# Eight tiles of a modulation's matrix-vector product on GpSimd instead of VectorE

## Chip, cores and metric

The kernel runs on one core of a Trainium2 chip. The metric is the device time in microseconds of one execution. Before the change it is 2267.84 us (median of three runs, 2267.05 to 2270.59).

## What is computed

Two transformer blocks run one after the other on 512 tokens of width 1024, in float32. The first block has two layers. Each layer begins with a modulation of a condition vector `c`:

```python
cond = jax.nn.silu(c)
for i in range(DEPTH):                       # 2 layers
    mod = (cond @ ada_w[i] + ada_b[i])[:, None, :]
    sh1, sc1, g1, sh2, sc2, g2 = jnp.split(mod, 6, axis=-1)
    h = rmsnorm(x, norm1_g[i]) * (1.0 + sc1) + sh1
    y = attention(h)                         # layer 0: sliding window, 16 query heads, 2 key heads
    x = x + g1 * y
    h = rmsnorm(x, norm2_g[i]) * (1.0 + sc2) + sh2
    x = x + g2 * swiglu(h, w_gate[i], w_up[i], w_down[i])
```

The second block (a gated convolution, a state space scan and a gated MLP) is not touched by the change.

## The kernel before

**Matrix products.** TensorE does each float32 product with three fp32r matmuls (lines 875, 877, 879): weight and activation are split into a high part, made by ScalarE (`whi`, line 1263), and a low part, made by VectorE (`wlo`, line 1572). The weights come as 360 units of 128x1024 through three buffers each of `raw`, `whi` and `wlo`. SyncE's queue loads `raw` (line 2090).

**The modulation.** There are 12 vectors of 1024 (`MODS`), j = 0 to 11, each the sum of 8 products of a 128x1024 tile of `ada_w` with a column of `cond`. A tile is n = 8j + k. Vectors 0 and 1 are made at the start by TensorE. The others (n = 16 to 95) are made by VectorE in `fma`: the first tile of a vector by a `tensor_scalar` (line 1587, output = tile x cond[k]), the others by a `scalar_tensor_tensor` (line 1590, acc = tile x cond[k] + acc). `modsum` (line 917) then sums over the partitions on TensorE, `modrows` copies the row on ScalarE, `modturn` (line 927) turns it to a column, `modadd` (lines 1612, 1617) adds the bias. j = 2 is `g1`, j = 3 and 4 are `sh2` and `sc2`, which the second norm needs. The accumulators are two: even j in slots 29 and 30, odd j in 31 and 32, so the first tile of a vector must wait until `modsum` has read the vector two before it. The tiles arrive in six buffers (`ada`, line 2103), and the load of a tile waits until the tile six before it has been multiplied.

**The order of work.** `score()` writes one list of ticks; each engine runs through it and does the ticks that are its own, in this order, waiting on semaphores. `mods()` yields one tile a step. Six tiles are woven into the first projection, 16 into the first attention (`queries()`), two into its output projection, the rest into the first MLP. In `queries()` there are 16 visits, two for each pair of heads t = 0 to 7; they are called visit 0 to 15 here. A visit runs, each for another item in flight, `exps`, `scores`, `turned`, `values`, then takes one tile from `mods()`; an even visit ends with `query` of the next t. Between two visits TensorE has three or four steps of a projection. On VectorE:
- `scores` adds the mask and takes the maxima (line 1832), then makes the negative maximum (lines 1836, 1838), for which ScalarE's `exps` (line 1436) waits. When the maxima are taken, the PSUM banks of the scores come free, and TensorE takes them again for what follows;
- `turned` of an odd visit: lines 1850, 1852, 1857 (a copy of the reciprocal denominators into a 128x512 tile);
- `values`: lines 1865 and 1568;
- `query`: line 1788 (head statistics from PSUM), then the rotation in lines 1798, 1802, 1804.

GpSimd takes the power -0.5 of those head statistics (line 2036) as soon as line 1788 is done, and later adds up the squares for the norms (line 2045).

Of the kernel before, what the change touches and what calls it, by code (L numbers as in the profile page):

```python
# [12 lines left out]
ALU = mybir.AluOpType  # L13
# [4 lines left out]
KD = D // P  # L18
# [7 lines left out]
NADA = 6  # L26
# [6 lines left out]
NEG = -1.0e30  # L33
EPS1 = 1e-6
EPS2 = 1e-5
MODS = [(0, 1), (0, 0), (0, 2), (0, 3), (0, 4), (0, 5)] + [(1, j) for j in range(6)]


# [61 lines left out]
class Score:  # L100
# [5 lines left out]
    def tick(self, *t):  # L106
        self.ticks.append(t)
# [93 lines left out]
def score():  # L201
    s = Score()
    tick, gemm = s.tick, s.gemm

    def column_sums(*js):

        tick("modsum", js)
        s.soon(3, "modrows", js)
        s.soon(7, "modturn", js)
        s.soon(9, "modadd", js)  # L210

    def mods():
        for j in range(2, 12):
            for k in range(KD):
                if k == 3 and j in (3, 6):
                    column_sums(j - 1)
                tick("fma", 8 * j + k)
                yield 1
            if j == 7:
                column_sums(6, 7)  # L220
                yield 1

# [65 lines left out]
    mod = mods()  # L288
# [364 lines left out]
def program(nc, ctx, io, ticks):  # L653
    def signal(name, by=1):
        return Signal(ctx.enter_context(nc.semaphore(name)), by)
# [13 lines left out]
        signal(f"a_{n}") for n in ("cut", "half", "ev", "sq", "att", "stick", "ssd"))  # L669
    v_cut, v_half, v_ev, v_mod, v_norm, v_res, v_att, v_stick, v_ssd, v_conv = (  # L670
        signal(f"v_{n}") for n in ("cut", "half", "ev", "mod", "norm", "res", "att", "stick", "ssd", "conv"))
    p_sum, p_pow, p_rope, p_ssd = (signal(f"p_{n}") for n in ("sum", "pow", "rope", "ssd"))
    sums_dram = nc.dram_tensor("sums", (32, S), F, kind="Internal").ap()
    ya_dram = nc.dram_tensor("ya", (KD, P, S), F, kind="Internal").ap()

# [175 lines left out]
    def tensor(e):  # L851
# [59 lines left out]
        def modsum(js):  # L911
            b = take(("mod", js))
            for n, j in enumerate(js):
                w.wait_ge(v_mod, ("fma", 8 * j + 7))
                for half in range(2):
                    g = 64 * n + 32 * half
                    i = e.matmul(b[g:g + 32, :], C("one").to_broadcast([P, 32]), modacc[j][:, S * half:S * half + S], start=True, stop=True,
                                 skip_group_check=True)
            i.then_inc(*t_mod.up(*js))
            give(("mod", js), a_att, ("modrows", js))  # L920
# [335 lines left out]
    def scalar(e):  # L1256
# [288 lines left out]
        for name, *a in ticks:  # L1545
            if name in do:
                do[name](*a)

    def item(n):

        return n // 8, n % 8 // 2, n % 2
# [11 lines left out]
    def vector(e):  # L1563
# [16 lines left out]

        def fma(n):
            j, k = divmod(n, KD)
            a, o = ada[(n - 16) % NADA], modacc[j]
            w.wait_ge(d_ada[(n - 16) % NADA], n)
            if k == 0:
                w.wait_ge(*((t_mod, j - 2) if 3 < j < 10 else (a_att, "cond")))
                e.tensor_scalar(o, a, cond[:, 0:1], None, ALU.mult).then_inc(*v_mod.up(("fma", n)))
            else:
                w.wait_ge(v_mod, ("fma", n - 1))
                e.scalar_tensor_tensor(o, a, cond[:, k:k + 1], o, ALU.mult, ALU.add).then_inc(*v_mod.up(("fma", n)))  # L1590
# [397 lines left out]
    def gpsimd(e):  # L1988
        w = Waits(e)
        TWO_PI = 2.0 * np.pi  # L1990
        C1 = 6.28125
        C2 = float(np.float32(round((TWO_PI - C1) * 2 ** 19) / 2 ** 19))
        C3 = float(TWO_PI - C1 - C2)
        MAGIC = 12582912.0
        LIM = 3.1415925
        steps = [0]

        def next_step(op):

            op.then_inc(*p_rope.up(steps[0]))  # L2000
            w.wait_ge(p_rope, steps[0])
            steps[0] += 1

        def reduce_angle(x, k, scale, shift):
            next_step(e.tensor_scalar(k, x, scale / TWO_PI, shift, ALU.mult, ALU.add))
            next_step(e.tensor_scalar(k, k, MAGIC, None, ALU.add))
            next_step(e.tensor_scalar(k, k, -MAGIC, None, ALU.add))
            for c in (C1, C2, C3):
                next_step(e.tensor_scalar(part, k, -c / scale, None, ALU.mult))
                next_step(e.tensor_tensor(x, x, part, ALU.add))  # L2010

        def angles():
            blocks = lambda ap: ap.rearrange("p (c r) -> p c r", c=4)
            w.wait_ge(d_in, "vec")
            w.wait_ge(d_pos, "pos")
            next_step(e.tensor_copy(part[:, 0:4], pos[:, :]))
            next_step(e.tensor_tensor(blocks(ang), blocks(C("invf")), part[:, 0:4].unsqueeze(2).to_broadcast([P, 4, 8]), ALU.mult))
            reduce_angle(ang, turn, 1.0 / 4096, 0.0)
            next_step(e.tensor_copy(ang2, ang))
            reduce_angle(ang2, turn, 1.0, 0.25)  # L2020
            next_step(e.tensor_scalar(ang2, ang2, float(np.pi / 2), None, ALU.add))

        def sine():
            reduce_angle(ang, turn, 1.0, 0.0)
            e.tensor_scalar(ang2, ang2, LIM, -LIM, ALU.min, ALU.max).then_inc(*p_rope.up("cos"))
            e.tensor_scalar(ang, ang, LIM, -LIM, ALU.min, ALU.max).then_inc(*p_rope.up("sin"))

        def pow_(sid):
            v, r = stat[sid]
            w.wait_ge(v_norm, ("scaled", sid))  # L2030
            e.tensor_tensor(r, v, C("half", 0, 4), ALU.pow).then_inc(*p_pow.up(sid))

        def head_pow(t):
            v, r = qstat[t]
            w.wait_ge(v_att, ("qstat", t))
            e.tensor_tensor(r, v, C("half", 0, 8), ALU.pow).then_inc(*p_pow.up(("q", t)))

        def add(sid, d):
            if 0 < d < nstat(sid):
                if d == 1:  # L2040
                    w.wait_ge(a_sq, (sid, 0))
                else:
                    w.wait_ge(p_sum, (sid, d - 1))
                w.wait_ge(a_sq, (sid, d))
                e.tensor_tensor(acc, acc, sq_of(sid, d), ALU.add).then_inc(*p_sum.up((sid, d)))  # L2045

        def sq(sid, d, last):
            if sid:
                add(sid, d)

        def per_head(ap, c, g):
            o = 32 * c + 8 * g
            return ap[:, o:o + 8].unsqueeze(2).to_broadcast([P, 8, 64])

        def h8(ap):
            return ap.rearrange("p (h r) -> p h r", h=8)

        def xrow(g, c):
            if c < 3:
                w.wait_ge(v_ssd, ("xd", g, c))  # L2060
                w.wait_ge(a_ssd, "dec")
                if g:
                    w.wait_ge(t_ssd, ("state", g - 1, c))
                e.tensor_tensor(h8(STMP[c]), h8(XD[c]), per_head(dec, c, g), ALU.mult).then_inc(*p_ssd.up(("st", g, c)))

        def masked(g, h):
            ex = EX[(8 * g + h) % 6]
            w.wait_ge(a_ssd, ("ex", g, h))
            w.wait_ge(a_ssd, ("x", 20 + g))
            e.tensor_tensor(ex[:, P:], ex[:, P:], Ct[g % 2][:, P:], ALU.mult).then_inc(*p_ssd.up(("ex", g, h)))  # L2070

        do = {"angles": angles, "sine": sine, "pow": pow_, "kstat": lambda: head_pow("k"), "query": head_pow, "sq": sq,
              "gadd": lambda i: add(("g", i // 4), i % 4), "xrow": xrow, "masked": masked}
        for name, *a in ticks:
            if name in do:
                do[name](*a)
# [2 lines left out]

    def sync(e):  # L2080
        w = Waits(e)
        loaded = [0, 16]

        def load():
            u = loaded[0]
# [6 lines left out]
        def ada_in(n):  # L2092
            j, k = divmod(n, KD)
            l, jj = MODS[j]
            return io["ada_w"][l, k * P:(k + 1) * P, jj * D:(jj + 1) * D]

        def fma(n):
            while loaded[1] < min(96, n + NADA):
                q = loaded[1]
                loaded[1] += 1  # L2100
                if q >= 16 + NADA:
                    w.wait_ge(v_mod, ("fma", q - NADA))
                e.dma_start(ada[(q - 16) % NADA], ada_in(q)).then_inc(*d_ada[(q - 16) % NADA].up(q))

        def evac(tile):
            if tile[0] == "spill":
# [40 lines left out]
                e.dma_start(early_part(q, k).rearrange("p (j c) -> p j c", j=2), parts[:, :, 256 * q:256 * q + 256]).then_inc(  # L2147
                    *d_early[q, k].up("in"))
        e.dma_start(cst[:, soon:], io["consts"][:, soon:]).then_inc(*d_late.up("in"))
        fma(13)  # L2150
        load()
        load()
        fma(16)
        def dtgain():
            w.wait_ge(v_mod, ("fma", 93))
            e.dma_start(wdt, io["wdt"]).then_inc(*d_wdt.up("in"))

        do = {"dtgain": dtgain, "lower": lambda u: load() if u > 2 else None, "fma": fma, "evac": evac, "dtturn": dtturn, "decay": lambda g, h: row(8 * g + h + 1), "fetch": fetch, "final": final}
        for name, *a in ticks:
            if name in do:  # L2160
                do[name](*a)
# [2 lines left out]
    engines = tensor, scalar, vector, gpsimd, sync  # L2164
    signals = [d_in, d_pos, d_out, *d_x, *d_raw, *d_ada, *d_early.values(), d_late, *d_ya, *d_row, d_sums, d_wdt, t_mm, t_mod, t_norm, t_att, t_stick, t_ssd, a_cut, a_half,
               a_ev, a_sq, a_att, a_stick, a_ssd, v_cut, v_half, v_ev, v_mod, v_norm, v_res, v_att, v_stick, v_ssd, v_conv, p_sum,
               p_pow, p_rope, p_ssd]
    for engine in engines:
        engine(Dry())
    for s in signals:  # L2170
# [89 lines left out]
```

## Time and profile before

| | |
|---|---|
| median of the runs | 2267.84 us |
| the profiled execution | 2267.9 us |
| its span, first to last instruction | 2265.9 us |
| TensorE busy | 2232.9 us (99%) |
| VectorE busy | 1193.5 us (53%) |
| ScalarE busy | 895.2 us (40%) |
| GpSimd busy | 165.0 us (7%) |
| granted TensorE clock, mean | 0.996 |

The time of the execution is 2.0 us longer than its span. "Busy" of TensorE counts pipelined matmuls whose ends are modelled, so what its rows show well are the gaps between them. A time such as 145.15 is in microseconds from the start of the span. "<-" behind a row names what released the instruction.

### The profile page before, as it was taken

To read this page: it belongs to the slowest core of one execution; us is meant where nothing else is said; L and a number is where in the kernel's file an instruction comes from. 1 tells how busy PE (TensorE), PEld (TensorE's weight loads), DVE (VectorE), ACT (ScalarE), POOL (GpSimd) and SP (SyncE) were. 2 spreads that over 40 slices of the span, in tenths; PEclk is the share of its full clock that TensorE was granted. 3 is DMA by queue.
4 is the path that set the end of the run, shared out by engine and by line. 5 is a ranking of instruction groups with operands and counts; after the bars stand their busy time and mean duration, and the time that the engine had idled before them with its cause. 6 is when DMAs were issued, how large, how long until landed. Compare 5 with 4: busy or idle time off the path is not lost. (4 is left out here: it accounts for less than half of the span.)

```text
span 2265.9 us, 26906 instructions
## 1 busy us (share of the span) xinstructions
PE 2232.9 (99%) x10904; PEld 1793.3 (79%) x10904; DVE 1193.5 (53%) x1651; ACT 895.2 (40%) x1445; POOL 165.0 (7%) x147
## 2 busy tenths in 40 slices
PE   8999999999999999999999999999999999999998
PEld 6766888888777778888888877887788888888886
DVE  4775755643465754333337446567752447553453
ACT  4654332223354533322333236367742224331331
POOL 2112000000000010000001001032210001000001
PEclk9999999999999999999999999999999999999999
DMA  9432555632212112232222324333333232333222
GB/s 332 149 121 84 215 212 207 215 108 93 84 57 75 57 68 94 93 103 102 94 84 98 107 75 154 103 103 112 102 114 115 84 111 85 102 94 102 93 84 84
DMA packets 82171, 258.72 MB, mean 114 GB/s; under 512 B 8800, under 2 KB 17376, under 8 KB 82048
## 3 DMA queue, kind: packets, MB, share of 16 engines
q1 hardware_dynamic: 82048, 257.01, 33.3%
q8 instruction: 86, 1.41, 0.3%
q14 instruction: 37, 0.30, 0.0%
HBM read 252.71 MB, written 4.26 MB: 113 GB/s over the span
## 5 line engine op out<-in xcount | busy, mean ns | idle before, releaser
L875 PE MATMUL pb<-hhi,whi 128*128 128x512 f32 x1936 | 767.3, 396 | 2.0 <-ACT hhi L1301 2.0
L877 PE MATMUL pb<-hhi,wlo 128*128 128x512 f32 x1936 | 754.3, 390 | 2.7 <-DVE wlo L1572 2.7
L879 PE MATMUL pb<-hlo,whi 128*128 128x512 f32 x1936 | 754.7, 390 | 0.0
L1572 DVE TENSOR_TENSOR wlo<-raw,whi 128x1024 fp32r<-128x1024 f32 x360 | 446.0, 1243 | 544.4 <-ACT whi L1263 544.3
L1263 ACT ACTIVATE whi<-raw 128x1024 fp32r<-128x1024 f32 x360 | 379.1, 1057 | 699.9 <-PE pb L879 675.3
L875 PEld LDWEIGHTS pb<-hhi,whi 128*128 128x128 f32 x1936 | 363.5, 188 | 88.3 <-issue 15.8
L877 PEld LDWEIGHTS pb<-hhi,wlo 128*128 128x128 f32 x1936 | 363.8, 188 | 78.9 <-DVE wlo L1572 4.1
L879 PEld LDWEIGHTS pb<-hlo,whi 128*128 128x128 f32 x1936 | 363.4, 188 | 77.9 <-DVE hlo L1669 1.3
L875 PE MATMUL pb<-ahi,whi 128*128 128x512 f32 x848 | 334.1, 394 | 1.6 <-ACT ahi L1459 0.9
L877 PE MATMUL pb<-ahi,wlo 128*128 128x512 f32 x848 | 330.2, 389 | 1.1 <-DVE wlo L1572 1.1
L879 PE MATMUL pb<-alo,whi 128*128 128x512 f32 x848 | 330.5, 390 | 0.0
L875 PEld LDWEIGHTS pb<-ahi,whi 128*128 128x128 f32 x848 | 159.2, 188 | 37.3 <-issue 4.2
L877 PEld LDWEIGHTS pb<-ahi,wlo 128*128 128x128 f32 x848 | 159.3, 188 | 34.4 <-DVE wlo L1572 1.5
L879 PEld LDWEIGHTS pb<-alo,whi 128*128 128x128 f32 x848 | 159.2, 188 | 34.1 <-DVE alo L1568 0.8
L2045 POOL TENSOR_TENSOR slab<-slab 128x512 f32<-128x512 f32 x46 | 69.4, 1508 | 1558.2 <-ACT slab L1280 1557.2
L1692 DVE SCALAR_TENSOR_TENSOR slab<-slab,vec 128x509 f32<-128x509 f32 (+2 forms) x132 | 99.0, 750 | 4.7
L1568 DVE TENSOR_TENSOR alo<-slab,ahi 128x512 fp32r<-128x512 f32 x90 | 62.3, 692 | 68.7 <-ACT ahi L1379 50.5
L1590 DVE SCALAR_TENSOR_TENSOR slab<-slab,small 128x1024 f32<-128x1024 f32 x70 | 90.6, 1295 | 1.9 <-DVE slab L1590 0.5
L1725 DVE TENSOR_TENSOR slab<-slab,pb 128x512 f32<-128x512 f32 x66 | 45.0, 683 | 47.6 <-PE pb L879 47.5
L1379 ACT ACTIVATE ahi<-slab 128x512 fp32r<-128x512 f32 x66 | 41.7, 632 | 68.7 <-DVE slab L1725 68.7
L1280 ACT ACTIVATE slab<-X 128x512 f32<-128x512 f32 x48 | 30.2, 629 | 82.7 <-DVE X L1701 35.0
L1877 DVE TENSOR_TENSOR_SCAN slab<-slab,cst 128x128 f32<-128x128 f32 (+3 forms) x64 | 52.2, 815 | 6.3 <-ACT slab L1472 6.3
(258 smaller groups left out, 1729.8 us busy)
## 6 DMA issues: line engine op xcount, KB each, us to landing
raw<-stream SPq DMA_DIRECT2D x360, 512.0 KB, 3.3
slab<-ada_w SPq DMA_DIRECT2D x80, 512.0 KB, 5.1
early<-ada_w SPq DMA_DIRECT2D x32, 256.0 KB, 8.1
slab<-sums SPq DMA_DIRECT2D x32, 256.0 KB, 4.2
X<-xT SPq DMA_DIRECT2D x8, 256.0 KB, 5.0
ya<-slab SPq DMA_DIRECT2D x8, 256.0 KB, 4.1
slab<-ya SPq DMA_DIRECT2D x8, 256.0 KB, 5.3
outT<-X SPq DMA_DIRECT2D x8, 256.0 KB, 2.1
```

Source lines behind the costliest of these rows:

```text
L875: e.matmul(out, wh, hi, start=s.k == 0, stop=False)
L877: e.matmul(out, wl, hi, start=False, stop=False)
L879: i = e.matmul(out, wh, lo, start=False, stop=s.last)
L1263: e.activation(whi[:, u % NW, :], raw[:, u % NRAW, :], ACT.Copy).then_inc(*a_cut.up(u))
L1379: e.activation(a_out[f % HALF][0], SG[f % 6], ACT.Copy).then_inc(*a_half.up(("f", l, f)))
L1568: e.tensor_tensor(out, src, hi.bitcast(F), ALU.subtract).then_inc(*v_half.up(key))
L1572: e.tensor_tensor(wlo[:, u % NW, :], raw[:, u % NRAW, :], whi[:, u % NW, :].bitcast(F), ALU.subtract).then_inc(*v_cut.up(u))
L1590: e.scalar_tensor_tensor(o, a, cond[:, k:k + 1], o, ALU.mult, ALU.add).then_inc(*v_mod.up(("fma", n)))
L1692: e.scalar_tensor_tensor(t[:, d:], u[:, :S - d], W(name, (width - 1 - d) * tiles + i), t[:, d:], ALU.mult, ALU.add).then_inc(*v_conv.up((k ...
L1725: e.tensor_tensor(t, t, b, ALU.mult).then_inc(*v_ev.up(tile))
L1877: e.tensor_tensor_scan(p[:, 0:wd][:, ::-1], RS[n % 4][:, 0:wd][:, ::-1], C("late", S - wd)[:, 0:wd][:, ::-1], 1.0, ALU.mult, ALU.max).then ...
L2045: e.tensor_tensor(acc, acc, sq_of(sid, d), ALU.add).then_inc(*p_sum.up((sid, d)))
```

## The change

The tiles n = 24 to 31 (j = 3) are made by GpSimd in a new tick `pool_fma`. Its first tile is one `tensor_scalar`; each other tile is a `tensor_scalar` in place in the `ada` buffer, a wait, and a `tensor_tensor` add into the accumulator. The order of the tiles becomes `MOD_ORDER`: 16 to 26, then 32, 27, 33, 28, 34, 29, 35, 30, 36, 31, 37, 38, 39, and then as before. So visits 2, 3, 4, 6, 8, 10, 12 and 14 of the attention take a GpSimd tile, and visits 0, 1, 5, 7, 9, 11, 13, 15 one of VectorE (22, 23, 32, 33, ... 37). As the first tile of j = 4 (n = 32) now comes in visit 5, the column sum of j = 2 moves from tile 27 to tile 26, and its copy follows after one product instead of three. Buffers and loads follow the place in `MOD_ORDER`.

```diff
+MOD_ORDER = [*range(16, 27), 32, 27, 33, 28, 34, 29, 35, 30, 36, 31, 37, 38, 39, *range(40, 96)]
...
     def column_sums(*js):
         tick("modsum", js)
-        s.soon(3, "modrows", js)
+        s.soon(1 if js == (2,) else 3, "modrows", js)
...
     def mods():
-        for j in range(2, 12):
-            for k in range(KD):
-                if k == 3 and j in (3, 6):
-                    column_sums(j - 1)
-                tick("fma", 8 * j + k)
-                yield 1
-            if j == 7:
+        for n in MOD_ORDER:
+            j, k = divmod(n, KD)
+            if n == 26 or n == 51:
+                column_sums(2 if n == 26 else 5)
+            tick("pool_fma" if j == 3 else "fma", n)
+            yield 1
+            if n == 63:
                 column_sums(6, 7)
                 yield 1
...
-                w.wait_ge(v_mod, ("fma", 8 * j + 7))
+                w.wait_ge(*multiplied(8 * j + 7))
...
+    def multiplied(n):
+        return (p_mod if n // KD == 3 else v_mod), ("fma", n)
...
+        def pool_fma(n):
+            j, k = divmod(n, KD)
+            at = MOD_ORDER.index(n) % NADA
+            a, o = ada[at], modacc[j]
+            w.wait_ge(d_ada[at], n)
+            if k == 0:
+                w.wait_ge(a_att, "cond")
+                e.tensor_scalar(o, a, cond[:, 0:1], None, ALU.mult).then_inc(*p_mod.up(("fma", n)))
+            else:
+                e.tensor_scalar(a, a, cond[:, k:k + 1], None, ALU.mult).then_inc(*p_mod.up(("scaled", n)))
+                w.wait_ge(p_mod, ("scaled", n))
+                e.tensor_tensor(o, o, a, ALU.add).then_inc(*p_mod.up(("fma", n)))
...
         def fma(n):
-            while loaded[1] < min(96, n + NADA):
-                q = loaded[1]
+            ada_load(MOD_ORDER.index(n) + NADA)
+
+        def ada_load(places):
+            while loaded[1] < min(len(MOD_ORDER), places):
+                place = loaded[1]
                 loaded[1] += 1
-                if q >= 16 + NADA:
-                    w.wait_ge(v_mod, ("fma", q - NADA))
-                e.dma_start(ada[(q - 16) % NADA], ada_in(q)).then_inc(*d_ada[(q - 16) % NADA].up(q))
+                q = MOD_ORDER[place]
+                if place >= NADA:
+                    w.wait_ge(*multiplied(MOD_ORDER[place - NADA]))
+                e.dma_start(ada[place % NADA], ada_in(q)).then_inc(*d_ada[place % NADA].up(q))
```

## Rows read from the trace of the kernel before

**Rows 1.** Busy time by stretch: us, PE, PEld, DVE, ACT, POOL, clock, DMA, GB/s
```profile
57.00:135.00 78.00, 77.87 (x518) 56.85 (x517) 61.37 (x174) 49.73 (x130) 14.06 (x7) 1.00 0.42 148
135.00:180.00 45.00, 39.67 (x275) 29.29 (x276) 30.17 (x95) 29.16 (x80) 4.02 (x2) 1.00 0.30 105
```
**Rows 2.** What TensorE waited for between 135 and 180 us (total, times, longest)
```profile
PE pb L1077 <- DVE small L1832: 3.2, 3, 1.1
PE pb L1063 <- DVE small L1832: 1.2, 2, 0.6
```
**Rows 3.** Timeline of TensorE: start, us, operation, idle before and its releaser
```profile
145.15 0.88 PE L1077 MATMUL pb<-slab 128*64 128x128 f32 x12 [1.10 <-DVE small L1832]
...
155.78 1.10 PE L1006 MATMUL pb<-slab,cst 128*128 128x512 f32 x2
...
170.14 1.13 PE L1049 MATMUL pb<-slab 64*128 64x256 f32 x8
...
200.84 1.05 PE L917 MATMUL pb<-slab,cst 128*32 128x512 f32 x4 [1.26 <-DVE slab L1590]
```
**Rows 4.** Timeline of VectorE in visits 9 to 15
```profile
129.02 0.16 DVE L1788 TENSOR_SCALAR small<-pb 128x8 f32<-128x8 f32 x1
...
132.51 0.16 DVE L1836 SCALAR_TENSOR_TENSOR small<-small 128x4 f32<-128x4 f32 x1
...
141.32 0.75 DVE L1587 TENSOR_SCALAR slab<-slab,small 128x1024 f32<-128x1024 f32 x1
...
155.85 1.28 DVE L1590 SCALAR_TENSOR_TENSOR slab<-slab,small 128x1024 f32<-128x1024 f32 x1
...
157.72 0.68 DVE L1802 TENSOR_TENSOR slab<-pb,slab 128x512 f32<-128x512 f32 x1
...
170.92 1.28 DVE L1590 SCALAR_TENSOR_TENSOR slab<-slab,small 128x1024 f32<-128x1024 f32 x1
172.12 0.41 DVE L1832 CUSTOM_DVE_ANT_0 slab<-pb,cst 128x256 f32<-128x256 f32 x1
```
**Rows 5.** Timeline of ScalarE: the exponentials of visit 9, a weight cut
```profile
132.91 0.60 ACT L1436 ACTIVATE slab<-slab,small 128x256 f32<-128x256 f32 x1 [3.04 <-DVE small L1838]
...
149.01 1.06 ACT L1263 ACTIVATE whi<-raw 128x1024 fp32r<-128x1024 f32 x1 [4.33 <-PE pb L879]
```
**Rows 6.** Timelines of GpSimd and of SyncE's queue in visits 8 and 9
```profile
129.25 2.01 POOL L2036 TENSOR_TENSOR small<-small,cst 128x8 f32<-128x8 f32 x1 [13.05 <-DVE small L1788]
...
128.31 1.14 SPq L2103 DMA_DIRECT2D slab<-ada_w  x2
```
**Rows 7.** By line: count, duration in ns min/median/max, first and last start
```profile
L2045 POOL TENSOR_TENSOR slab<-slab x46: 1277/1299/2163, 196.2 to 2248.1; 128x512 f32<-128x512 f32 x46
...
L2070 POOL TENSOR_TENSOR slab<-slab x17: 1002/1020/1990, 1390.0 to 1652.8; 128x384 f32<-128x384 f32 x17
...
L2009 POOL TENSOR_SCALAR slab<-slab x9: 287/288/718, 5.8 to 20.1; 128x32 f32<-128x32 f32 x9
...
L1617 DVE SCALAR_TENSOR_TENSOR small<-small,vec x3: 169/169/740, 208.3 to 603.1; 128x8 f32<-128x8 f32 x3
...
L1798 DVE TENSOR_TENSOR slab<-slab x8: 677/680/682, 63.9 to 157.1; 128x512 f32<-128x512 f32 x8
...
L1651 DVE SCALAR_TENSOR_TENSOR hlo<-X,vec,hhi x16: 751/1272/1550, 1180.6 to 1897.0; 128x512 fp32r<-128x512 f32 x16
```
**Rows 8.** Timelines of VectorE and GpSimd where both work on SBUF
```profile
208.32 0.74 DVE L1617 SCALAR_TENSOR_TENSOR small<-small,vec 128x8 f32<-128x8 f32 x1
...
207.29 1.74 POOL L2045 TENSOR_TENSOR slab<-slab 128x512 f32<-128x512 f32 x1 [3.14 <-ACT slab L1280]
...
1183.41 1.28 DVE L1651 SCALAR_TENSOR_TENSOR hlo<-X,vec,hhi 128x512 fp32r<-128x512 f32 x1 [1.44 <-ACT hhi L1284]
...
1182.84 1.30 POOL L2045 TENSOR_TENSOR slab<-slab 128x512 f32<-128x512 f32 x1 [337.31 <-ACT slab L1280]
```

More of the change, by code:

```diff
@@ L671, in program @@
         signal(f"v_{n}") for n in ("cut", "half", "ev", "mod", "norm", "res", "att", "stick", "ssd", "conv"))
-    p_sum, p_pow, p_rope, p_ssd = (signal(f"p_{n}") for n in ("sum", "pow", "rope", "ssd"))
+    p_sum, p_pow, p_rope, p_ssd, p_mod = (signal(f"p_{n}") for n in ("sum", "pow", "rope", "ssd", "mod"))
     sums_dram = nc.dram_tensor("sums", (32, S), F, kind="Internal").ap()
@@ L1582, in fma @@
             j, k = divmod(n, KD)
-            a, o = ada[(n - 16) % NADA], modacc[j]
-            w.wait_ge(d_ada[(n - 16) % NADA], n)
+            at = MOD_ORDER.index(n) % NADA
+            a, o = ada[at], modacc[j]
+            w.wait_ge(d_ada[at], n)
             if k == 0:
@@ L2036, in head_pow @@
             e.tensor_tensor(r, v, C("half", 0, 8), ALU.pow).then_inc(*p_pow.up(("q", t)))
+        def pool_fma(n):
+            j, k = divmod(n, KD)
+            at = MOD_ORDER.index(n) % NADA
+            a, o = ada[at], modacc[j]
+            w.wait_ge(d_ada[at], n)
+            if k == 0:
[5 more added lines that the diff above has]
+                e.tensor_tensor(o, o, a, ALU.add).then_inc(*p_mod.up(("fma", n)))
         def add(sid, d):
@@ L2070, in masked @@
             e.tensor_tensor(ex[:, P:], ex[:, P:], Ct[g % 2][:, P:], ALU.mult).then_inc(*p_ssd.up(("ex", g, h)))
-        do = {"angles": angles, "sine": sine, "pow": pow_, "kstat": lambda: head_pow("k"), "query": head_pow, "sq": sq,
+        do = {"angles": angles, "sine": sine, "pow": pow_, "kstat": lambda: head_pow("k"), "query": head_pow, "pool_fma": pool_fma, "sq": sq,
               "gadd": lambda i: add(("g", i // 4), i % 4), "xrow": xrow, "masked": masked}
@@ L2081, in sync @@
         w = Waits(e)
-        loaded = [0, 16]
+        loaded = [0, 0]
         def load():
@@ L2149, in sync @@
         e.dma_start(cst[:, soon:], io["consts"][:, soon:]).then_inc(*d_late.up("in"))
-        fma(13)
+        ada_load(3)
         load()
         load()
-        fma(16)
+        ada_load(NADA)
         def dtgain():
@@ L2156, in dtgain @@
             e.dma_start(wdt, io["wdt"]).then_inc(*d_wdt.up("in"))
-        do = {"dtgain": dtgain, "lower": lambda u: load() if u > 2 else None, "fma": fma, "evac": evac, "dtturn": dtturn, "decay": lambda g, h: row(8 * g + h + 1), "fetch": fetch, "final": final}
+        do = {"dtgain": dtgain, "lower": lambda u: load() if u > 2 else None, "fma": fma, "pool_fma": fma, "evac": evac, "dtturn": dtturn, "decay": lambda g, h: row(8 * g + h + 1), "fetch": fetch, "final": final}
         for name, *a in ticks:
@@ L2166, in program @@
                a_ev, a_sq, a_att, a_stick, a_ssd, v_cut, v_half, v_ev, v_mod, v_norm, v_res, v_att, v_stick, v_ssd, v_conv, p_sum,
-               p_pow, p_rope, p_ssd]
+               p_pow, p_rope, p_ssd, p_mod]
     for engine in engines:
```

## The prediction

> **What bounds the kernel now.** I read the busy times first. TensorE is busy nearly all the time, so an edit on VectorE can only win what TensorE stands idle for on its account. The table by stretch shows where that is. From 57 to 135 us TensorE is busy 77.87 of 78 us; from 135 to 180 us, when the output projection has begun, it is busy 39.67 of 45 us [rows 1]. The 5.3 us between are the most that the visits can give. TensorE's waits in that stretch name VectorE: 3.2 us before `values` and 1.2 us before `turned`, both released by the maxima of line 1832 [rows 2]. TensorE's timeline puts the three large ones in visits 11, 13 and 15, each about 1.1 us, the first at 145.15 [rows 3]. The banks of the scores are free only when the maxima are taken, and in odd visits VectorE is late with these: ahead of them it does, in one row, the tile of the even visit, line 1788 and the rotation [rows 4]. One more idle of TensorE belongs to the modulation: 1.26 us before `modsum` of j = 3 and 4 at 200.84, released by tile 39 [rows 3]. Tile 39 stays on VectorE, so this wait stays.
>
> **What the change takes away.** VectorE loses eight tiles: tile 24, a `tensor_scalar` of 0.75 us, and seven of 1.28 us; visit 5 changes from a long to a short one and visit 10 loses a short one. That is some 9 us of VectorE's work. What counts is what lies ahead of the three waits.
> - Visit 10 loses 0.75 us, 0.66 to the start of the next instruction (141.32, [rows 4]). TensorE's wait in visit 11 shrinks by 0.66 us.
> - Visit 12 loses 1.28 us at 155.85. But the rotation there needs TensorE's turn, which ends at 155.78 + 1.10 = 156.88 [rows 3]; line 1802 started at 157.72 [rows 4], so the row of work moves up by 0.8 us at most.
> - Visit 14 loses 1.28 us at 170.92. The maxima behind it began at 172.12 [rows 4]; their scores end at 170.14 + 1.13 = 171.27 [rows 3]. That is 0.8 us.
>
> Sum: 0.66 + 0.8 + 0.8 = 2.3 us gained. The tiles of visits 2 to 8 win nothing: TensorE did not wait there [rows 1].
>
> **What the change adds on GpSimd.** The add: 128x384 takes 1.00 us and 128x512 takes 1.28 us undisturbed [rows 7], which is 2.15 ns a column; 1024 columns are 1.28 + 512 x 0.00215 = 2.4 us. The `tensor_scalar` of 1024 columns is not in the trace. Its lower bound is the 0.29 us of 32 columns [rows 7], its upper the add's 2.4 us. It reads 1024 elements a partition, as many as an add of 512 columns does, so I take the 1.3 us of that row. A tile then costs GpSimd some 3.8 us, between 2.7 and 4.8. The Trainium skill, page GPSIMD Engine Reference, section "Engine selection", says that one-input operations on GpSimd are roughly line-rate; by that an estimate would be 0.9 us for the scaling and 3.3 us for the tile. No run so far shows it.
>
> GpSimd has nothing else to do between two powers, which lie 13 us apart [rows 6], and its tile is loaded long before: the loads at 128.31 [rows 6] are for tiles five places ahead. So it does not keep to its visit; each tile starts right behind the power of line 2036, one visit or more early (two tiles, 7.6 us, behind the second power). No power is made late, and SyncE's loads, which now wait for GpSimd's tiles of six places before, find them done. I cost both at nothing; if a tile took over 10 us the powers would become late and with them the scores.
>
> **What it costs VectorE.** The two engines get in each other's way. At 208.32 a `scalar_tensor_tensor` of 8 columns on VectorE takes 0.74 us and not 0.17, and ends as the add on GpSimd ends that started at 207.29 [rows 7, 8]. At 1183.41 line 1651 takes 1.28 us, not 0.75, beside an add that ran from 1182.84 [rows 7, 8]: VectorE stood until about 0.2 us before the add's end, then did its 0.75 us. So a VectorE instruction with two SBUF inputs that meets a running add waits for all of it. The powers do not do this: line 1798 runs beside each of them and always takes 0.68 us [rows 7].
>
> Now place it. Line 1788 of visit 8 starts at 129.02 and moves to 127.8. The power runs to 130.1, the scaling to 131.4, the add to 133.9. Line 1836, two SBUF inputs, stood at 132.51 [rows 4] and would come at 131.3, line 1838 at 131.5: one of the two meets the scaling's end or the add. The negative maximum, for which ScalarE's exponentials were already waiting at 132.91 [rows 5], comes between 132.5 and 134, so between 0.4 us earlier and 1.2 later; I take +0.8. ScalarE's chain behind it (exponentials, evacuations, weight cut) feeds VectorE's line 1572, and so the wait of visit 11: +0.8 us. The same pattern follows in visit 11, where the stall of 2.2 us (an add less 0.2) meets slack: ScalarE stood there until 149.01 for TensorE anyway [rows 5]; the VectorE tile behind it is late, and I put +0.3 on TensorE. In visit 13 the exponentials again follow the negative maximum at once; 2.2 us less the 0.8 moved up, with 0.4 of slack before the next bank is wanted: +1.0. After visit 14 GpSimd has no tile left. Sum: 0.8 + 0.3 + 1.0 = 2.1 us lost.
>
> The Trainium skill, page SBUF — State Buffer, section "Who interferes with whom", says that a copy or a `tensor_scalar` on VectorE that runs in a two-port mode blocks in the same way. By that, line 1857 and the tiles of line 1587 would stall as well; no row here shows one beside a GpSimd add. As line 1857 stands behind line 1836, it would mostly come after the same add, and the sum would move by at most one more stall.
>
> **Other edits.** The column sum of j = 2 comes two visits earlier, into the stretch where TensorE has no wait; its tiles are ready, its four matmuls are the same. It shifts which PSUM bank follows which; bounded by +-0.6 us, the size of one bank wait in [rows 2], taken as zero. Tile 32 needs that sum to have been read, a visit earlier: no wait.
>
> **The sum.** -2.3 + 2.1 = -0.2 us on the profiled execution, 2267.9 us, which stands 0.06 us above the median of the runs. Forecast 2267.7 us.
>
> **Rivals.**
> - *Traded evenly* (forecast): each stall of VectorE eats what the removed tile gave. 2266.0 to 2270.0 with the bounds of the scaling and of the overlaps. Chance 0.62.
> - *VectorE wins the ports*: its short instructions slip in between and GpSimd waits. Then only the 2.3 us stay: 2265.6. For it: the powers never disturb. Against it: all of [rows 8]. Chance 0.15.
> - *The lock on the path* (slower): in visits 9, 11 and 13 the add always starts before line 1836, and nothing hides it. 3 x 2.2 - 2.3 = +4.3 us, 2272.2; with the scaling (1.1 us each) blocking as well, +7.6 us, 2275.5. It decides from the point where GpSimd's scaling ends before VectorE's maxima do. For it: ScalarE waits on exactly this value [rows 5]. Against it: slack in visit 11. Chance 0.15.
> - *VectorE's lateness was all*: with 9 us less work, all 5.3 us of idle in 135 to 180 go: 2262.6. Against it: the bounds by TensorE's own turn and scores above. Chance 0.04.
> - *It does not do what it says*: GpSimd's tiles take so long that powers or `modsum` wait for them; over 10 us a tile, some 2270 and more. Chance 0.04.
>
> **How the numbers follow.** A measurement of this kernel tells about 0.2%, 4.5 us, from no change. The first two cases and the lower half of the third are within it. Faster by more: the fourth, 0.04. Slower by more: half of the third and part of the last, 0.09. Same: 0.87. The range takes in the first two cases and the nearer end of the third, and a margin for the runs' own spread (2267.05 to 2270.59): 2264.0 to 2272.5.
>
> **What the profile after would show.** VectorE busy without stalls would fall by 9 us; with mine it falls less, as stalled rows count as busy. Rows of lines 1836, 1838, 1850 or 1857 longer than 0.5 us show the lock; if all stay at 0.17, the second case holds. GpSimd's tiles should start right behind the powers, with adds of 2.4 us or more. The wait of visit 15 should shrink to 0.3 us; those of 11 and 13 hardly in sum. I am wrong if TensorE gets new waits before 135 us, or if the powers move.

## The result, and the profile after

The changed kernel takes **2278.12 us** (median of 6 runs, 2277.23 to 2280.42). The kernel before took 2269.14 us beside it. The ratio is 1.0038, with a 95% interval of 1.0028 to 1.0048: the change costs 9 us. The forecast was 2267.7 us, within 2264.0 to 2272.5, and was wrong. The profiled execution took 2280.42 us, its span is 2278.5 us.

First the same two stretches as in [rows 1] and three short ones (window, length, busy time of TensorE, its weight loads, VectorE, ScalarE and GpSimd, granted clock, share of the DMA engines, GB/s):

```profile
57.00:135.00 78.00, 73.37 (x460) 53.55 (x460) 57.45 (x150) 45.30 (x118) 35.99 (x15) 0.98 0.37 129
135.00:180.00 45.00, 38.76 (x264) 27.97 (x263) 35.86 (x94) 24.28 (x68) 21.89 (x9) 0.94 0.32 111
123.00:129.00 6.00, 6.00 (x35) 4.12 (x31) 3.67 (x9) 2.10 (x4) 1.45 (x1) 0.72 0.00 0
153.00:159.00 6.00, 5.01 (x24) 3.88 (x24) 5.79 (x14) 0.53 (x1) 5.34 (x3) 0.72 0.55 218
179.00:185.00 6.00, 6.00 (x31) 4.61 (x29) 2.20 (x7) 3.91 (x10) 0.00 (x0) 0.77 0.30 102
```

Before the change TensorE stood idle 0.1 us of the first stretch [rows 1]; now it stands 4.6 us there. The granted clock, 1.00 in both stretches of [rows 1], is 0.72 to 0.77 in three windows of 6 us: part of each ran at the lower of the two levels, 1.2 GHz. What TensorE waited for from 57 to 250 us, largest first (total, times, longest):

```profile
PE pb L1078 <- DVE small L1618: 3.4, 1, 3.4
PE pb L1064 <- DVE small L1838: 2.9, 2, 2.3
PE pb L1078 <- DVE small L1838: 1.8, 3, 1.1
PE pb L918 <- DVE slab L1596: 1.2, 1, 1.2
PE pb L1078 <- ACT spare L1324: 1.2, 1, 1.2
```

Lines 1064, 1078 and 1838 are 1063, 1077 and 1832 of before. Two names are new against [rows 2]: line 1618, `modadd`, which adds the bias to a column sum, and line 1324, `modrows`, which copies its row. Both waits belong to the column sum of j = 2, not to GpSimd. TensorE's timeline places them:

```profile
98.36 1.05 PE L918 MATMUL pb<-slab,cst 128*32 128x512 f32 x4
...
104.66 0.88 PE L1078 MATMUL pb<-slab 128*64 128x128 f32 x12 [1.21 <-ACT spare L1324]
...
114.44 0.46 PE L928 MATMUL pb<-cst,spare 64*128 64x64 f32 x4
...
122.36 0.88 PE L1078 MATMUL pb<-slab 128*64 128x128 f32 x12 [3.43 <-DVE small L1618]
123.16 0.50 PE L876 MATMUL pb<-hhi,whi 128*128 128x512 f32 x1
123.50 0.40 PE L878 MATMUL pb<-hhi,wlo 128*128 128x512 f32 x1
123.73 0.57 PE L880 MATMUL pb<-hlo,whi 128*128 128x512 f32 x1
124.10 0.63 PE L876 MATMUL pb<-hhi,whi 128*128 128x512 f32 x1
...
153.99 1.09 PE L1078 MATMUL pb<-slab 128*64 128x128 f32 x12 [1.10 <-DVE small L1838]
...
169.80 0.88 PE L1078 MATMUL pb<-slab 128*64 128x128 f32 x12 [0.46 <-DVE small L1838]
...
177.15 0.65 PE L1064 MATMUL pb<-cst,slab 128*128 128x128 f32 x4 [2.31 <-DVE small L1838]
...
212.96 1.05 PE L918 MATMUL pb<-slab,cst 128*32 128x512 f32 x4 [1.25 <-DVE slab L1596]
```

The bank that `modsum` filled at 98.36 is wanted again by `values` of visit 5, before ScalarE has copied the row. The bank that `modturn` filled at 114.44 is wanted by `values` of visit 7, before VectorE has added the bias. And 1.7 us after this 3.43 us wait the product that took 0.40 us takes 0.63: the granted clock fell to the lower level after TensorE had stood. Why the bias comes so late is in the timeline of VectorE and GpSimd in visit 7:

```profile
118.85 0.42 DVE L1838 CUSTOM_DVE_ANT_0 slab<-pb,cst 128x256 f32<-128x256 f32 x1
...
119.11 2.84 POOL L2053 TENSOR_SCALAR slab<-slab,small 128x1024 f32<-128x1024 f32 x1
...
120.34 0.17 DVE L1842 SCALAR_TENSOR_TENSOR small<-small 128x4 f32<-128x4 f32 x1
120.54 0.17 DVE L1844 TENSOR_TENSOR small<-small 128x4 f32<-128x4 f32 x1
...
121.13 1.10 DVE L1863 COPY spare<-small 128x512 f32<-128x512 f32 x1
122.03 2.42 POOL L2055 TENSOR_TENSOR slab<-slab 128x1024 f32<-128x1024 f32 x1
122.15 0.15 DVE L1618 TENSOR_TENSOR small<-pb,vec 128x8 f32<-128x8 f32 x1
122.22 3.31 DVE L1596 SCALAR_TENSOR_TENSOR slab<-slab,small 128x1024 f32<-128x1024 f32 x1
```

In VectorE's order the bias stands behind the rotation, the maxima and the copy of a whole visit, and comes 7.7 us after the turn. In the kernel before it comes at 126.61, 4.0 us after the turn at 122.60, and the rotation's first step (line 1788) follows at 129.02 [rows 4]. GpSimd adds little to it: the copy took 1.10 us instead of 0.43. The tile product behind it met the add and took 3.31 us instead of 1.28, but TensorE has no further wait until 145.50.

**The balance.** Executions differ by some 1.6 us before the first visit, so I count from the first head statistics (line 999) to `modsum` of j = 3 and 4 (the last of TensorE's rows above): 62.09 to 212.96, 150.87 us. In the kernel before it is 60.40 to 200.84, 140.44 us. Up to 132.89 (125.18 before) the difference is 6.0 us: the waits of 1.2 and 3.4 us, and 1.5 us for seven products at the lower clock (0.43 us apart, not 0.23) and the scores behind them. Behind it are another 4.4 us: two more low stretches after the waits at 153.99 and 177.15 (1.3 and 0.9 us), new waits of 0.9 and 1.7 us (the second is the 2.31 in the place of 0.59), less gains of 0.6 and 0.8 us at visits 13 and 15. That is 3.4 us. Another 0.9 us is the lower clock again, in the matmuls that stand between these two waits and the products (at 153.99 line 1078 takes 1.09 us, at 169.80 the same shape 0.88). The last 0.2 us has no row. The median of the runs shows 9 us and not 10.4: the profiled execution is the slowest of the six.

### The profile page after: what moved, and what is told of

The parts are those of the page before. It is cut to its first block and busy times, and to the rows that moved or that the text cites. A ratio compares the mean times of both kernels' runs of the same rounds, so it can differ in the third digit from the quotient of the medians.

```text
span 2278.5 us, 26908 instructions
## 1 busy us (share of the span) xinstructions
PE 2240.0 (98%) x10904; PEld 1797.8 (79%) x10904; DVE 1201.3 (53%) x1643; ACT 895.0 (39%) x1445; POOL 204.7 (9%) x162
```

## The experiments

My theory after the result: the earlier column sum costs the time, by its two bank waits. The rival: GpSimd's work costs it, by holding up VectorE's instructions.

**The change without GpSimd, and GpSimd without the new order.** In e1 VectorE makes all tiles, in the changed order:

```diff
-            tick("pool_fma" if j == 3 else "fma", n)
+            tick("fma", n)
```

> The new order of tiles and the moved column sum, but all tiles on VectorE. Theory A (the moved column sum): the two new waits of TensorE, 3.4 us for the bank that the bias addition of j = 2 frees and 1.2 us for the bank that its row copy frees, stay or grow by the tile that is back on VectorE; 2273 to 2276 us, against about 2269 for the kernel before. Theory B (GpSimd's lock on the ports): no GpSimd tile, so no loss; 2268 to 2270 us.

In e2 GpSimd makes j = 3, but the tiles, the column sum and its steps are in the order of before:

```diff
-MOD_ORDER = [*range(16, 27), 32, 27, 33, 28, 34, 29, 35, 30, 36, 31, 37, 38, 39, *range(40, 96)]
+MOD_ORDER = [*range(16, 96)]
...
-            if n == 26 or n == 51:
+            if n == 27 or n == 51:
...
-        s.soon(1 if js == (2,) else 3, "modrows", js)
+        s.soon(3, "modrows", js)
```

> GpSimd makes j = 3, but the tiles keep the order of before and the column sum of j = 2 stays at tile 27. A: the new bank waits are gone; 2267 to 2271 us. B: the stalls of copies and tiles beside GpSimd stay where visits 3 to 9 have them; if these are the cause, 2273 to 2278 us.

Measured: e1 2280.0 us, ratio 1.0042 (1.0027 to 1.0057). e2 2271.62 us, 1.0005 (0.9996 to 1.0014). The whole loss is there without GpSimd and gone with it in the old order. The rival falls as the cause of the loss. e1 came out 4 us above its expectation: beside the two waits, now 4.0 and 1.2 us, a third one grew (1.5 us on line 1794 for 0.4 in the changed kernel), and the granted clock from 135 to 180 us is 0.92, not 0.94.

**Which part of the new order.** e5 is the kernel before with one edit: the column sum of j = 2 one tile earlier (with its row after one product).

> The order of tiles of before and all tiles on VectorE; only the column sum of j = 2 (sum, copy, turn, bias addition) comes one tile earlier, as in the changed kernel. If this move alone makes the loss, TensorE waits 1.2 us and about 4 us for its two banks and the time is 2277 to 2281 us. If the loss needs the new order of tiles too, under 2274 us.

Measured: 2277.73 us, 1.0033 (1.0020 to 1.0046). So this one edit costs 7.5 us (4.5 to 10.4), most of the loss if not all. Its waits and its clock in TensorE's timeline:

```profile
106.48 0.88 PE L1078 MATMUL pb<-slab 128*64 128x128 f32 x12 [1.21 <-ACT spare L1324]
...
124.70 1.34 PE L1078 MATMUL pb<-slab 128*64 128x128 f32 x12 [3.95 <-DVE small L1618]
125.97 0.80 PE L876 MATMUL pb<-hhi,whi 128*128 128x512 f32 x1
```

From the first head statistics to those of visit 10 it needs 85.00 us (63.90 to 148.90), before 78.41 (60.40 to 138.81). That is 6.6 us more, and the rows account for it: waits 1.21 + 3.95, and 1.55 for the seven groups from 124.70 to 128.55, which take 3.85 us and not the 2.30 of before.

**Which step of the sum.** e3 is the changed kernel with the turn and the bias later; e6 has the bias earlier instead, right behind the turn.

```diff
-        s.soon(7, "modturn", js)
-        s.soon(9, "modadd", js)
+        s.soon(11 if js == (2,) else 7, "modturn", js)     # e3
+        s.soon(13 if js == (2,) else 9, "modadd", js)      # e3
+        s.soon(7 if js == (2,) else 9, "modadd", js)       # e6, turn unchanged
```

> The changed kernel with one edit: the turn and the bias addition of j = 2 come four products later, at the place that they had before. A: the 3.4 us wait goes, and with it the stretch at the lower TensorE clock behind it (about 1.5 us); 2272 to 2274 us. B: no change, 2277 to 2279 us.

> The changed kernel, with the bias addition of j = 2 in the list right behind its turn, ahead of the rotation and the maxima of visit 7, instead of two products later. If TensorE waits for a bank that this short VectorE instruction frees, the 3.4 us wait goes and the time is 2271 to 2274 us, as with the later turn; if it is the turn's own place on TensorE that costs, it stays at 2277 us or more.

Measured: e3 2272.47 us, 1.0012 (1.0003 to 1.0021); e6 2273.48 us, 1.0013 (1.0004 to 1.0023). Either edit takes the wait on line 1618 away and gives back about 5 us, more than the 3.4 us of the wait. The granted clock of both profiles is 1.00 from 97 to 137 us, where the changed kernel's is 0.96. So it is the place of the bias in VectorE's order that costs, and not the place of the turn in TensorE's.

**What GpSimd's work costs.** From e3, three kernels. e7 shrinks the GpSimd tiles 25 to 31 to 8 columns, e8 only their scalings. e4 stands on the changed kernel and puts a second scaling in the place of the add. In these three the vector j = 3 is not the sum of its tiles.

```diff
-                e.tensor_scalar(a, a, cond[:, k:k + 1], None, ALU.mult)...
+                e.tensor_scalar(a[:, 0:8], a[:, 0:8], cond[:, k:k + 1], None, ALU.mult)...        # e7, e8
-                e.tensor_tensor(o, o, a, ALU.add)...
+                e.tensor_tensor(o[:, 0:8], o[:, 0:8], a[:, 0:8], ALU.add)...                      # e7
+                e.tensor_scalar(o, a, cond[:, k:k + 1], None, ALU.mult)...                        # e4
```

> The kernel with the later turn (2272.5 us), and GpSimd's tiles 25 to 31 shrunk from 1024 to 8 columns (j = 3 is then not the sum of its tiles; tile 24 stays whole): VectorE is relieved and nothing is blocked. The difference to the kernel with the later turn is the whole price of GpSimd's port use. If that is what eats the gain: 2267 to 2269.5 us, 3 to 5 us below it. If the blocking is hidden: 2271.5 us or more.

> The kernel with the later turn, with GpSimd's scalings of tiles 25 to 31 shrunk to 8 columns and the adds whole (j = 3 is then wrong). The adds now start right behind the powers, 2.9 us earlier, and meet line 1842 (1836 before), the negative maximum. If a stall there is worse than one behind it, as the prediction had it, above 2272.5 us; if only the length of the blocking counts, 2269 to 2272 us.

> The changed kernel, with GpSimd's add replaced by a second scaling into the accumulator (j = 3 is then not the sum of its tiles). Tells what a scaling blocks. If a running scaling blocks VectorE instructions with two SBUF inputs, as the page says of every GpSimd instruction that reads SBUF, VectorE's tiles 33 to 36 take 3.7 us each, longer than the 3.3 us beside the add, and the time stays 2277 to 2280 us. If it blocks only copies and tensor_scalar, as the rows of the changed kernel look, the tiles take 1.28 us, the 2.3 us wait of visit 14 shrinks to under 1 us, and the time is 2275 to 2277 us.

Measured: e7 2267.93 us, 0.9989 (0.9979 to 0.9998); e8 2268.61 us, 0.9992 (0.9982 to 1.0001); e4 2274.43 us, 1.0019 (1.0009 to 1.0028). With e3 at 2272.47, GpSimd's work costs 4.5 us against e7; the adds alone cost 0.7, which the intervals don't resolve. So the offload would be worth 2.75 us (0.5 to 4.8 by the interval) if GpSimd stalled nobody, where the first term of the forecast has 2.3. Six of the seven adds of e8 fall where the forecast had put its stalls, on the negative maximum, which then takes 1.3 to 1.6 us. VectorE and GpSimd in e8:

```profile
131.46 2.39 POOL L2055 TENSOR_TENSOR slab<-slab 128x1024 f32<-128x1024 f32 x1
...
132.29 1.57 DVE L1842 SCALAR_TENSOR_TENSOR small<-small 128x4 f32<-128x4 f32 x1
133.90 0.17 DVE L1844 TENSOR_TENSOR small<-small 128x4 f32<-128x4 f32 x1
```

The scaling ahead of the add moves the add 2.9 us later, away from the small instructions and onto the large ones. This is how the changed kernel gets its 2.31 us wait in visit 14 (VectorE and GpSimd in the changed kernel):

```profile
170.90 0.83 DVE L1863 COPY spare<-small 128x512 f32<-128x512 f32 x1
...
171.54 2.44 POOL L2055 TENSOR_TENSOR slab<-slab 128x1024 f32<-128x1024 f32 x1
...
171.66 3.41 DVE L1577 TENSOR_TENSOR wlo<-raw,whi 128x1024 fp32r<-128x1024 f32 x1
174.98 1.27 DVE L1596 SCALAR_TENSOR_TENSOR slab<-slab,small 128x1024 f32<-128x1024 f32 x1
...
176.26 0.28 DVE L1838 CUSTOM_DVE_ANT_0 spare<-pb,cst 128x128 f32<-128x128 f32 x1
```

The weight split takes 3.41 us and not 1.22. The maxima of the next visit stand behind it and free their banks late. In e4, which has no add, this wait is 0.9 us, and e4 came out below both of its expectations.

**Can the scaling be had elsewhere?** e9 is e3 with ScalarE scaling the tiles, one tile ahead, and GpSimd only adding. e10 is e3 with `modrows` right behind `modsum`. e11 has both.

```diff
+        def prescale(n):                                                                  # e9, e11
...
+            e.activation(a, a, ACT.Copy, scale=cond[:, n % KD:n % KD + 1])...
...
-        s.soon(1 if js == (2,) else 3, "modrows", js)
+        tick("modrows", js) if js == (2,) else s.soon(3, "modrows", js)                   # e10, e11
```

> The changed kernel with the later turn and bias (2272.47 us when it ran), and with the scaling of tiles 25 to 31 moved from GpSimd to ScalarE, one tile ahead and in place; GpSimd only adds (tile 24 stays as it was). Port theory: the 2.85 us scaling is what pushes the add onto VectorE's tile and weight split, so this runs like the kernel with adds only (2268.61), 2268 to 2269.5 us, with the adds now right behind the powers. ScalarE theory: ScalarE already ends visit 11's wait with its rounding of a weight tile, so 7 more instructions of about 1.1 us (its 128x1024 rounding takes 1057 ns) on it make new waits on the rounded weights or on the squares, and the time stays at 2271 or goes over 2273 us.

> The changed kernel with the later turn and bias, and with ScalarE's copy of the second modulation's row out of its PSUM bank put right behind the matmuls that fill it. Bank theory: the 1.2 us wait of the values' product of visit 5 on that copy goes, so 2271.3 us, 1.2 below 2272.5. Other theory: TensorE is only late in another place (ScalarE's evictions behind the copy are pushed by its 0.6 us, and the next wait grows), so 2272 to 2273 us.

> Both edits of the two kernels before this one together. If the two gains add up: 2267 to 2268.5 us, at or under the kernel before by 0.1%. If ScalarE can't take the scalings, no better than 2271 us.

Measured: e9 2271.86 us, 1.0008 (0.9999 to 1.0017); e10 2272.41, 1.0008 (0.9999 to 1.0016); e11 2270.98, 1.0008 (0.9999 to 1.0017). None reaches the time of e8 (2268.61). In e10 the 1.2 us wait on the row is gone from the profile; from e3 to e10 the ratio falls by 0.0004, 0.9 us, which the intervals don't resolve. In e11 ScalarE's seven scalings take 1.15 us each, the adds run right behind the powers and make VectorE's small instructions (line 1842 of the changed kernel) take up to 2.17 us, and the largest waits that are left are these:

```profile
PE pb L1082 <- DVE small L1847: 2.4, 3, 1.1
PE pb L1068 <- DVE small L1847: 2.2, 2, 1.7
```

(lines 1078, 1064 and 1838 of the changed kernel): 4.6 us, where before has 4.4 [rows 2].

**The order of the tiles, and the forecast's own case.** e12 is e3 with all tiles on VectorE. e13 is the changed kernel with the column sum of j = 2, its row, turn and bias left where they were. e15 is e13 with all tiles on VectorE, e14 is e13 with ScalarE scaling.

```diff
-            if n == 26 or n == 51:
-                column_sums(2 if n == 26 else 5)
+            if n == 32 or n == 51:
+                column_sums(2 if n == 32 else 5)
...
-        s.soon(1 if js == (2,) else 3, "modrows", js)
+        s.soon(3, "modrows", js)
```

> All 16 tiles on VectorE in the new order of tiles, the column sum one tile earlier, the turn and the bias later, nothing of it on GpSimd. Against the same with GpSimd (2272.5) this is GpSimd's net share. If the new order and sum cost only by the banks' waits, this is within 1.5 us of the kernel before plus the 1.2 us wait on the row: 2270 to 2272 us. If the new order of tiles has a cost of its own, 2273 us or more.

> The changed kernel with the column sum of j=2, its row, turn and bias where they were before (ahead of the twelfth tile, after 3, 7 and 9 products); GpSimd and the alternating tiles stay as changed. If the forecast was wrong only in the column sum, this gives what the forecast's sum gave without it: 2269.9 - 0.2, so 2268.5 to 2271 us. If GpSimd's use of VectorE's ports (3.4 us tile products and weight splits, the 2.3 us wait of visit 14) costs more than the offload gains, 2272 us or more.

> The new order of tiles alone: everything on VectorE, column sum where it was. If the order of tiles is free, the kernel before within its scatter, 2269 to 2271 us. If it has a cost of its own (the tile of j=3 and of j=4 need other loads), 2272 us or more.

> The same with the scaling of tiles 25 to 31 on ScalarE, so that GpSimd only adds. If the 2.85 us scaling on GpSimd keeps the gain of 2.75 us away, this is the fastest legal version: 2267 to 2268.5 us, 0.1% under the kernel before. If the adds or ScalarE's lateness keep it away too, 2269.5 to 2271 us.

Measured: e12 2272.33 us, 1.0011 (1.0002 to 1.0020). e13 2271.42, 1.0006 (0.9997 to 1.0015). e15 2270.73, 1.0003 (0.9994 to 1.0012). e14 2273.33, 1.0015 (1.0006 to 1.0024). The pairs e3 and e12, e13 and e15 differ by GpSimd alone: 0.1 and 0.7 us, within the scatter of both. With the sum left in place no loss is measurable: e13 lies 1.6 us above the kernel before (-0.7 to +3.4). e14 is above both of its expectations: ScalarE's scaling in visit 5 makes the row's copy late, and TensorE waits for it:

```profile
113.96 1.05 PE L1003 MATMUL pb<-cst,slab 128*128 128x2 f32 x8 [1.18 <-ACT spare L1333]
```

Of the twelve of these kernels that compute the whole result none is measurably faster than the kernel before.

## Why the prediction was wrong

**The step that failed is the column sum of j = 2.** The forecast said that it comes "into the stretch where TensorE has no wait", bounded it by +-0.6 us and took zero. It measured +7.5 us by itself (e5). (It also said that the sum moves two visits; it moves one, from visit 5 to visit 4, as e5 has it.) A stretch without waits is no stretch with slack: the banks go round in the order in which they are asked for, and the matmul that gets the sum's bank waits for whoever empties it. The right question was where, in VectorE's and ScalarE's order, the bias and the row's copy stand: the first cost a wait of 3.43 us, gone in e3 and e6, the second one of 1.21 us, gone in e10. The bound was also wrong in kind: it was the size of a wait on another line, not the length of the queue ahead of this one.

**The clock was not in the sum at all.** After some of the waits matmuls ran at 1.2 GHz, which took 1 to 2 us of extra time each; in e5 that is 1.55 of the 6.6 us, in the changed kernel some 4.6 us in the three stretches. It is read from rows; no run isolated it, and nothing here says what would have kept the clock up.

**Right in size, in part by luck: the gain.** 2.3 us forecast, 2.75 in e7. By visits: visit 13 waits 0.46 us for 1.10, visit 15 0.20 us for 0.99, as worked out. Visit 11 still waits 1.10 us, in e7 too, where GpSimd does almost nothing; there the 0.66 us were not won. In their place the two waits ahead of `turned` in visit 11 (0.41 and 0.54 us in the kernel before) are gone in e7, which the forecast had not named; and e7 carries the 1.21 us wait on the row.

**Mis-sized and in another place: the lock.** 2.1 us forecast. It is 4.5 us in the pair e7 and e3, and where the forecast had put it, on the negative maximum, it is 0.7 us (e8 against e7), which is not resolved. The net of the two terms held nevertheless: e12 to e3 and e15 to e13, where GpSimd's work and its relief come together, give 0.1 and 0.7 us, near the forecast's -0.2. With both terms made up otherwise than forecast, that is luck. The stalls are not on lines 1836 and 1838 (1842 and 1844 now; min/median/max of the first 164/165/167 ns). They are on the copy, the tile products and the weight split:

```profile
L1596 DVE SCALAR_TENSOR_TENSOR slab<-slab,small x12: 1271/1284/3387, 55.9 to 187.9; 128x1024 f32<-128x1024 f32 x12
...
L1863 DVE COPY spare<-small x8: 430/1000/1183, 90.8 to 194.8; 128x512 f32<-128x512 f32 x8
...
L1577 DVE TENSOR_TENSOR wlo<-raw,whi x10: 1212/1220/3406, 61.7 to 195.1; 128x1024 fp32r<-128x1024 f32 x10
...
L1593 DVE TENSOR_SCALAR slab<-slab,small x1: 2877/2877/2877, 106.2 to 106.2; 128x1024 f32<-128x1024 f32 x1
```

The last row is tile 32, the `tensor_scalar` of line 1587 before, which took 0.75 us there. The forecast had named this line and the copy as ones that might stall too; both did. The rival in which VectorE wins the ports falls with these rows. The reason for the other place is the next term.

**Mis-sized: the scaling.** I took 1.3 us, from an add of 512 columns, and a bound of 2.4. It takes 2.85 us, more than the add of 1024 columns (2.42, forecast 2.4), so a tile takes 5.3 us and not 3.8:

```profile
L2053 POOL TENSOR_SCALAR slab<-slab,small x7: 2842/2845/2852, 88.6 to 168.6; 128x1024 f32<-128x1024 f32 x7
...
L2055 POOL TENSOR_TENSOR slab<-slab x7: 2387/2417/2443, 91.5 to 171.5; 128x1024 f32<-128x1024 f32 x7
```

The Trainium skill, page GPSIMD Engine Reference, section "Engine selection", calls one-input operations roughly line-rate; the estimate of 0.9 us that the forecast worked out from it does not hold here, the measurement decides.

**Confirmed: the tiles start right behind the powers** (power 117.09, scaling 119.11, add 122.03), and the powers are not late through them. The forecast had also named the sign of its error, new waits of TensorE before 135 us.

**The range.** It ended at 2272.5, and nothing in it stood for moving the sum beyond the +-0.6 us. With the sum left in place, e13 lies at 2271.42 us and within the range. Part of its distance from the forecast is the base: the forecast counts from 2267.9 us, and the kernel before measured 2269.1 to 2270.7 us beside the changed kernel and the experiments.

## What to carry to other kernels

When an edit moves a step that takes a buffer from a ring, look up who empties that buffer and what stands ahead of that engine's step in its own order; absence of waits in the stretch says nothing about it. Split a change into its parts on the chip before explaining it: here the part that was meant to help was neutral, and the small reordering that made room for it cost most of the 9 us (7.5 by itself). An operation put on GpSimd needs a row of its own kind and size, since its length sets the time of GpSimd's next instruction, and with it which of VectorE's that one stalls.

## What the hardware showed

**A GpSimd scaling holds off two-input reads only at its start.** In e4 a tile product that started at 120.78 beside a scaling begun at 120.60 took 2.06 us, not 1.28: 0.8 us more, while the scaling ran on to 123.49. Two more like it took 2.13 us each. A tile product that started 1.5 us behind the start of a scaling (79.47 and 77.94) took its 1.28 us. Lines 1842 and 1844 ran in 0.17 us in the middle of a scaling (rows at 120.34 above). A copy is held to the scaling's end: 121.13 + 1.10 against 119.11 + 2.84. Once it was the other way round: a weight split that began at 168.98, 0.11 us behind a scaling, took its 1.21 us, and the scaling took 3.94. The rows of e4:

```profile
77.94 2.85 POOL L2051 TENSOR_SCALAR slab<-slab,small 128x1024 f32<-128x1024 f32 x1
...
79.47 1.28 DVE L1596 SCALAR_TENSOR_TENSOR slab<-slab,small 128x1024 f32<-128x1024 f32 x1
...
119.67 1.12 DVE L1863 COPY spare<-small 128x512 f32<-128x512 f32 x1
120.60 2.89 POOL L2055 TENSOR_SCALAR slab<-slab,small 128x1024 f32<-128x1024 f32 x1
...
120.78 2.06 DVE L1596 SCALAR_TENSOR_TENSOR slab<-slab,small 128x1024 f32<-128x1024 f32 x1
```

The Trainium skill, page SBUF — State Buffer, section "Who interferes with whom", lets a VectorE instruction with two SBUF inputs contend with any GpSimd instruction that reads SBUF, and names the copy among those that can run in a two-port mode, in which whoever comes second blocks for the whole instruction. The copy agrees (1.10 us instead of 0.43). The two-input rule agrees beside an add (3.31 us instead of 1.28) but only for the first microsecond beside a scaling.

**Half a microsecond more of waiting, three more of time.** e12 and e15 have a wait of 0.95 and 0.99 us ahead of `turned` in visit 11 where the kernel before has 0.41, and in the 10 us behind it (147 to 157) the granted clock is 0.66 and 0.84. From the head statistics of visit 10 to the next ones e12 needs 19.53 us (141.71 to 161.24), before 16.17 (138.81 to 154.98): 3.4 us, of which the wait is 0.54 and the products at 0.63 us the rest. The row of e12 behind the waits:

```profile
148.60 1.55 PE L1078 MATMUL pb<-slab 128*64 128x128 f32 x12 [1.10 <-DVE small L1838]
150.07 0.80 PE L876 MATMUL pb<-ahi,whi 128*128 128x512 f32 x1
150.67 0.63 PE L878 MATMUL pb<-ahi,wlo 128*128 128x512 f32 x1
```

The profile of e3, where this wait is 0.35 us, keeps 1.00 from 137 to 177 us, and that of the kernel before too. The size of the wait alone doesn't decide: e3 and e13 have the same 2.30 us wait in visit 14, and behind it e3 keeps 1.00, while e13 shows 0.66 from 167 to 177 us. Where the clock falls and where it doesn't is not settled by these runs.
